# x added by VectorE, rotations of the scan on GpSimd, x scaled before its transposes, states used in groups of four

## The reference, cut to what matters

```python
h = rms_norm(x, norm_mix_g)
a_val, a_gate, u, g_conv, g_ssm = split(h @ w_in)              # 768, 768, 256, 1024, 1024 columns
v = silu(layer_norm(depthwise_conv31(a_val * sigmoid(a_gate)) + conv_b))
y_conv = v @ w_conv_out
s[t] = a * s[t-1] + B u[t]                                     # complex, 16 groups of 64 states
y = gelu(real(C s) + d_skip * u);  y_ssm = (y * sigmoid(y @ w_glu + b_glu)) @ w_ssm_out
x = x + (sigmoid(g_conv) * y_conv + sigmoid(g_ssm) * y_ssm) @ w_out
h = rms_norm(x, norm_ffn_g)
top_v, top_e = top_k(h @ w_router + b_router, 4);  gate = softmax(top_v)
for e in experts of a token:                                   # w_gate_up[e]: 1024 x 2048, w_down[e]: 1024 x 1024
    g, lin = split(h @ w_gate_up[e] + b_gate_up[e])
    x += gate_e * ((min(g, 7) * sigmoid(1.702 g) * (clip(lin, -7, 7) + 1)) @ w_down[e] + b_down[e])
out = rms_norm(x, norm_final_g)
```

## Time and profile before

| | us |
|---|---|
| median of three runs (lowest, highest) | 1112.43 (1111.92, 1113.12) |
| the profiled execution, its own time | 1112.21 |
| its span | 1110.5 |
| busy in the span: TensorE, VectorE, ScalarE, GpSimd | 1060.8, 284.6, 165.6, 75.3 |
| HBM traffic over the span | 389 GB/s, 432 MB |

### The profile page before, as it was taken

The page is one execution under the profiler, slowest core; times in us unless marked ns, Lnnn a source line. Parts: engine busy times, 40 slices in busy tenths (PEclk is TensorE's granted clock), DMA queues, the critical chain, the costliest instruction groups (busy, mean ns, idle before and its releaser), DMA issues.

```text
span 1110.5 us, 12064 instructions
## 1 busy us (share of the span) xinstructions
PE 1060.8 (96%) x4951; PEld 457.2 (41%) x4952; DVE 284.6 (26%) x661; ACT 165.6 (15%) x296; POOL 75.3 (7%) x153
## 2 busy tenths in 40 slices
PE   7999999999999999999999999999999999999996
PEld 6888784533333333333333333333333333333332
DVE  6999751311111111111111111111101111111112
ACT  3011301211111111111111111101001111111103
POOL 3975000000000000000000000000000000000000
PEclk9999999999999999999999999999999999999999
DMA  7853488799999999999999999999999999999995
GB/s 226 281 158 146 185 347 358 285 427 426 431 436 427 432 431 431 434 433 433 428 432 432 429 432 431 432 432 430 433 432 431 433 431 431 429 431 428 422 423 235
DMA packets 43035, 432.07 MB, mean 389 GB/s; under 512 B 5647, under 2 KB 21437, under 8 KB 24604
## 3 DMA queue, kind: packets, MB, share of 16 engines
q1 hardware_dynamic: 43004, 431.64, 92.9%
HBM read 430.58 MB, written 1.05 MB: 389 GB/s over the span
## 4 chain that ended last, share of the span: by engine, by line
PE 60%; DMA 26%; DVE 10%; ACT 1%; issue 1%; another core or an unknown queue 1%; SPq 1%; DVEq 0%
PE bank L1483 30%; DMA ring<-w_gate_up 22%; PE bank L1495 13%; DVE bank L936 6%; PE bank L1504 4%; PE bank L1445 4%; DMA ring<-w_down 3%; PE bank L1410 2%; PE bank L1375 2%; ACT area L722 1%; PE bank L1451 1%; PE bank L1476 1%; DVE bank L971 1%; DMA ring<-ssm_b_im 1%
## 5 line engine op out<-in xcount | busy, mean ns | idle before, releaser
L1483 PE MATMUL bank<-ring,area 128*64 128x512 f32 x2048 | 455.9, 602 | 22.3 <-DMA ring<-w_gate_up 22.3
L1483 PEld LDWEIGHTS bank<-ring,area 128*64 128x64 f32 x2048 | 149.4, 139 | 311.8 <-issue 272.5
L1495 PE MATMUL bank<-ring,area 128*64 128x512 f32 x1024 | 227.4, 595 | 6.1 <-ACT area L722 2.6
L1102 DVE TENSOR_SCALAR area<-bank 128x512 f32<-128x512 f32 x32 | 22.1, 692 | 732.6 <-PE bank L1483 732.6
L1495 PEld LDWEIGHTS bank<-ring,area 128*64 128x64 f32 x1024 | 72.0, 137 | 141.2 <-issue 131.7
L1264 PE MATMUL bank<-area,ring 128*128 128x256 f32 x480 | 106.6, 381 | 2.2 <-DMA ring<-w_in 2.2
L1264 PEld LDWEIGHTS bank<-area,ring 128*128 128x128 f32 x480 | 90.3, 190 | 17.1 <-DMA ring<-w_in 2.7
L728 ACT ACTIVATE area<-area 128x512 f32<-128x512 f32 x32 | 20.2, 632 | 486.9 <-DVE area L1102 486.9
L936 DVE SCALAR_TENSOR_TENSOR bank<-ring,spread,bank 128x256 f32<-128x256 f32 x174 | 71.5, 483 | 0.6
L1445 PE MATMUL bank<-rows,pick 128*64 128x512 f32 x256 | 63.6, 618 | 0.4 <-DVE onehot L1091 0.4
L1504 PE MATMUL bank<-area,spT 64*128 64x512 f32 x248 | 61.6, 615 | 0.7 <-ACT area L725 0.7
(11 more groups left out here) (243 smaller groups left out, 492.3 us busy)
## 6 DMA issues: line engine op xcount, KB each, us to landing
ring<-w_gate_up SPq DMA_DIRECT2D x47, 4096.0 KB, 48.9
ring<-w_down SPq DMA_DIRECT2D x26, 4096.0 KB, 46.6
ring<-w_gate_up SPq DMA_DIRECT2D x19, 2048.0 KB, 18.3
ring<-w_gate_up SPq DMA_DIRECT2D x30, 1024.0 KB, 12.0
ring<-w_down SPq DMA_DIRECT2D x18, 1024.0 KB, 21.2
ring<-w_in SPq DMA_DIRECT2D x15, 1024.0 KB, 8.0
ring<-w_down SPq DMA_DIRECT2D x3, 2048.0 KB, 10.8
ring<-w_out SPq DMA_DIRECT2D x1, 4096.0 KB, 14.2
```

The lines of the kernel that those rows point to most:

```text
L1102: return v.tensor_scalar(gc, bank[4][:, :], 7.0, None, ALU.min)
L1483: last = mm(bank[4 + b][64 * h:64 * h + 64, :], heT[:, k % 4, k // 4 * 64:k // 4 * 64 + 64], fours(w, b, h), start=False, stop=(k == KD - 1))
L1495: last = mm(bank[b][64 * h:64 * h + 64, :], src[:, k % 4, k // 4 * 64:k // 4 * 64 + 64], w[:, k % 2, h * 512:h * 512 + 512], start=(k == 0 ...
```

## The change

What it does, from the front to the end:

- VectorE and ScalarE scale one tile of x each by its reciprocal root into `x_rows`, TensorE transposes that, and the two engines share the eight blocks of hT, with the gain alone. A few products without use (`keep_busy`) stand where the transposes stood. One more small DMA brings norm_ffn_g into the parameter rows.
- VectorE writes the second product of a scan step into `rot`, and GpSimd takes the two sums of step t-1 behind its turning of step t; the last step's stay with VectorE. TensorE uses the states in two groups of four (`y_quad`).
- The gain of the second norm goes into w_router (`wrt_ready`, on VectorE ahead of the SSM gating) and, for the experts, into the copy of the transposed tokens (`by_gain_T`, VectorE instead of ScalarE). The broadcast of norm_ffn_g over all partitions is gone; w_router, b_router and the gain are issued behind w_out. Rows, logits and masks no longer lie in the slots of expert 1's chunks 6 to 8, which are issued earlier.
- x is no longer put into the banks by TensorE before the output products: VectorE adds it to their sums (`add_rows`), and the sum goes into the banks by four identity products (`residual`) behind expert 15. The output products of tile 1 run one half of the columns after the other, and its transposes and logits in two parts.
- Tokens are gathered with a stride, and ScalarE's copy `hrow` undoes it. Expert 27 is loaded in sets of four chunks.

```diff
-END = {E - 5: (4, 2, 2, 4), E - 4: (4, 2, 2, 4), E - 3: (4, 2, 1, 1, 4),
+END = {E - 4: (4, 2, 2, 4), E - 3: (4, 2, 1, 1, 4),
...
-WARM = 8, 2, 6, 3
+WARM = 1, 4, 6, 3
...
+        rot = [grid(at(23, 512, 512 * i), 2, T) for i in range(2)]
         ygelu, yglu = grid(at(11, 512), 2, T), grid(at(11, 512, 512), 2, T)
...
+            sp.dma_start(par_rows[r0:r0 + KD, :], norm_ffn_g[0].rearrange("(k p) -> k p", p=128)).then_inc(par_in, 16)
...
             sp.wait_ge(y_pe, ST)
-            sp.dma_start(gffn, norm_ffn_g.to_broadcast([128, D])).then_inc(ffn_in, 16)
-            sp.dma_start(wrt, w_router[0].rearrange("(p k) n -> p k n", p=128)).then_inc(ffn_in, 16)
-            sp.dma_start(brow, b_router.to_broadcast([128, E])).then_inc(ffn_in, 16)
+            load(1, 7, 1)
+            load(1, 8, 1)
...
             load_over_win((3, 4, 5, 0))
             sp.wait_ge(biasb_ready, 1)
             sp.dma_start(wout, w_out[0].rearrange("(k p) n -> p k n", p=128)).then_inc(wout_in, 16)
+            sp.dma_start(wrt, w_router[0].rearrange("(k p) n -> p k n", p=128)).then_inc(ffn_in, 16)
+            sp.dma_start(brow, b_router.to_broadcast([128, E])).then_inc(ffn_in, 16)
+            sp.dma_start(gain[:, :], norm_ffn_g[0].rearrange("(p k) -> p k", p=128)).then_inc(ffn_in, 16)
             load_over_win((1, 2))
             for h in range(2):
                 sp.dma_start(bdown[h], b_down[0, :, h * 512:h * 512 + 512]).then_inc(down_in, 16)
...
             load(1, 9, 1)
+            sp.wait_ge(mixed, 4)
+            load(1, 6, 1)
             for j in (1, 2, 3, 4):
                 sp.wait_ge(wout_used, j)
                 load(1, j, 1)
             load(1, 5, 1)
-            sp.wait_ge(logits_pe, TT)
-            load(1, 6, 1)
-            sp.wait_ge(top8, TT)
-            load(1, 7, 1)
-            sp.wait_ge(gates_ready, TT)
-            load(1, 8, 1)
...
+                if t >= 1:
+                    pool.wait_ge(rot_ready, t)
+                    x_, r_ = xs[(t - 1) % NX], rot[(t - 1) % 2]
+                    g.tensor_tensor(x_[:, 0, :], x_[:, 0, :], r_[:, 1, :], ALU.subtract)
+                    g.tensor_tensor(x_[:, 1, :], x_[:, 1, :], r_[:, 0, :], ALU.add).then_inc(states, 1)
 
...
+            act.wait_ge(rstd_x, 1)
+            s.activation(x_rows[:, 0, :], x_sb[:, 0, :], ACT.Copy, scale=rstd[:, 0:1]).then_inc(x_scaled, 1)
             act.wait_ge(params_pe, 1)
             s.activation(par[:, :], bank[7][:, 0:54], ACT.Copy).then_inc(params_sb, 1)
-            act.wait_ge(spread_pe, 1)
-            s.activation(rstd_all, bank[6][:, 0:T], ACT.Copy).then_inc(rstd_sb, 1)
...
+            for b in (1, 3):
+                act.wait_ge(xT_pe, b + 1)
+                for k in (2 * b, 2 * b + 1):
+                    s.activation(hT[:, k, :], bank[b][:, k % 2 * T:k % 2 * T + T], ACT.Copy, scale=p_g[:, k:k + 1]).then_inc(hT_act, 1)
...
+            square(0, 0)
+            square(0, 1)
+            act.wait_ge(h2T_pe, 1)
+            s.activation(h2T[:, 0:4, :], grid(bank[4][:, :], 4, 128), ACT.Copy).then_inc(h2T_act, 1)
+            root_and_exp(0)
+            s.activation(area[:, 1464:1466], ident[:, 0:2], ACT.Sqrt)
+            square(1, 0)
+            act.wait_ge(h2T_pe, 3)
+            act.wait_ge(logits_pe, 1)
+            s.activation(h2T[:, 0:4, :], grid(bank[6][:, :], 4, 128), ACT.Copy).then_inc(h2T_act, 1)
+            square(1, 1)
+            act.wait_ge(h2T_pe, 4)
+            s.activation(h2T[:, 4:6, :], grid(bank[7][:, 0:256], 2, 128), ACT.Copy).then_inc(h2T_act, 1)
+            root_and_exp(1)
+
...
-                return s.activation(hrow, bank[6][:, :], ACT.Copy)
-
-            def h_T_copy():
-                return s.activation(heT, grid(bank[7][:, :], 4, 128), ACT.Copy)
+                return s.activation(grid(hrow, 4, 128), bank[6][:, :].rearrange("a (p m) -> a m p", m=4), ACT.Copy)
...
-            link(v.reciprocal(rstd, rstd))
-            dve.wait_ge(consts, 1)
-            for t in range(TT):
-                v.tensor_scalar(diag[:, t, :], ident[:, :], rstd[:, t:t + 1], None, ALU.mult).then_inc(diag_ready, 1)
+            v.reciprocal(rstd, rstd).then_inc(rstd_x, 1)
+            dve.wait_ge(rstd_x, 1)
+            v.tensor_scalar(x_rows[:, 1, :], x_sb[:, 1, :], rstd[:, 1:2], None, ALU.mult).then_inc(x_scaled, 1)
...
-            dve.wait_ge(rstd_sb, 1)
-            for k in range(KD):
-                v.scalar_tensor_tensor(hT[:, k, :], bank[k // 2][:, k % 2 * T:k % 2 * T + T], p_g[:, k:k + 1],
-                                       rstd_all, ALU.mult, ALU.mult).then_inc(hT_ready, 1)
+            for b in (0, 2):
+                dve.wait_ge(xT_pe, b + 1)
+                for k in (2 * b, 2 * b + 1):
+                    v.tensor_scalar(hT[:, k, :], bank[b][:, k % 2 * T:k % 2 * T + T], p_g[:, k:k + 1], None, ALU.mult).then_inc(hT_dve, 1)
...
+                dve.wait_ge(rawT_pe, 1)
+                if t >= 1:
+                    dve.wait_ge(rot_ready, t)
...
+                if t >= 2:
+                    dve.wait_ge(states, t - 1)
...
                 v.tensor_tensor(xs[t % NX], zz, cb, ALU.mult)
-                link(v.tensor_tensor(zz, zz, sb_, ALU.mult))
-                v.tensor_tensor(xs[t % NX][:, 0, :], xs[t % NX][:, 0, :], zz[:, 1, :], ALU.subtract)
-                v.tensor_tensor(xs[t % NX][:, 1, :], xs[t % NX][:, 1, :], zz[:, 0, :], ALU.add).then_inc(states, 1)
-
+                v.tensor_tensor(rot[t % 2], zz, sb_, ALU.mult).then_inc(rot_ready, 1)
+                if t == ST - 1:
+                    dve.wait_ge(rot_ready, ST)
+                    v.tensor_tensor(xs[t % NX][:, 0, :], xs[t % NX][:, 0, :], rot[t % 2][:, 1, :], ALU.subtract)
+                    v.tensor_tensor(xs[t % NX][:, 1, :], xs[t % NX][:, 1, :], rot[t % 2][:, 0, :], ALU.add).then_inc(states, 1)
                 taps_of(order[scanning + SCAN_TAPS * t:scanning + SCAN_TAPS * (t + 1)])
-                dve.wait_ge(states, t + 1)
...
             v.tensor_copy(biasb[0:32, :], bias32[0:32, :]).then_inc(biasb_ready, 1)
+            dve.wait_ge(ffn_in, 48)
+            v.tensor_tensor(wrt, wrt, gain_k.unsqueeze(2).to_broadcast([128, KD, E]), ALU.mult).then_inc(wrt_ready, 1)
...
-            def weighed_by_k(t):
-
...
-                    v.tensor_tensor(dst[:, p, :], grid(gffn[:, c], 64, KD), grid(bank[2 * t + h][:, :], 64, KD),
-                                    ALU.mult).then_inc(h_ready, 1)
+            def add_rows(t, h):
+
+                r = rows[:, t, h * 512:h * 512 + 512]
+                v.tensor_tensor(r, bank[2 * t + h][:, :], r, ALU.add).then_inc(h_ready, 1)
...
+            def by_gain_T():
+
+                both = gain[:, :].rearrange("p (h m) -> p m h", h=2).unsqueeze(3).to_broadcast([128, 4, 2, CAP])
+                return v.tensor_tensor(heT.rearrange("p m (h c) -> p m h c", h=2),
+                                       bank[7][:, :].rearrange("p (m h c) -> p m h c", m=4, h=2), both, ALU.mult)
...
+                keep_busy(4)
+            pe.wait_ge(x_sq, TT)
+            keep_busy(2)
+            pe.wait_ge(par_in, 16 * 10)
...
+            tr(bank[7][:, 0:62], par_rows[:, :], ident[0:62, 0:62]).then_inc(params_pe, 1)
+            pe.wait_ge(x_scaled, TT)
+            for k in range(KD):
+                for t in range(TT):
+                    last = tr(bank[k // 2][:, k % 2 * T + t * 128:k % 2 * T + t * 128 + 128],
+                              x_rows[:, t, k * 128:k * 128 + 128], ident[:, :])
+                if k % 2:
+                    last.then_inc(xT_pe, 1)
...
-            y_pair(0)
+            y_quad(0)
             project(12)
-            y_pair(2)
             project(13)
-            y_pair(4)
             project(14, (0,))
-            y_pair(6)
-
+            y_quad(4)
...
-                if j == 1:
-
-                    pe.wait_ge(ssm_gated, 4)
-                    for n in range(4):
-                        mm(bank[n][:, :], ident[:, :], x_sb[:, n // 2, n % 2 * 512:n % 2 * 512 + 512], start=True, stop=False)
...
             pe.wait_ge(wout_in, 16)
-            pe.wait_ge(ffn_in, 48)
-            for t in range(TT):
+            pe.wait_ge(wrt_ready, 1)
+            pe.wait_ge(ssm_gated, 4)
...
+            def out_product(t, k, h):
+
+                pe.wait_ge(mixed, k // 2 + 1)
+                return mm(bank[2 * t + h][:, :], gateC[:, k, t * 128:t * 128 + 128], wout[:, k, h * 512:h * 512 + 512],
+                          start=(k == 0), stop=(k == KD - 1))
+
+            for k in range(KD):
+                for h in range(2):
+                    last = out_product(0, k, h)
+            last.then_inc(x1_pe, 1)
+            for h in range(2):
                 for k in range(KD):
-                    pe.wait_ge(mixed, k // 2 + 1)
-                    for h in range(2):
...
+                    last = out_product(1, k, h)
+                    if h == 1 and k % 2:
                         last.then_inc(wout_used, 1)
...
+                    if (h, k) == (0, 3):
```

(10 more changed lines are left out.)

233 lines of the change are left out of this document (112 added, 121 removed).

## The result

The changed kernel takes 1117.44 us (median of 5 runs, 1116.33 to 1117.78), the kernel before 1112.55 (1111.92 to 1113.12): ratio 1.0043, 95% interval 1.0033 to 1.0054. It is slower by 4.9 us; the forecast was 1.4 faster. The profiled execution took 1116.33, span 1114.5, so 4.0 more span than before.

What follows compares the result with a forecast made beforehand. The weight stream at 431 GB/s, started by expert 0's first refill, sets the end. Terms +0.1 + 1.7 + 0.45 - 2.6 - 1.2 + 0.15 = -1.4 on 1112.2, plus 0.2 for the median, gave 1111.0 us; range 1103.0 to 1115.5.

Steps and rivals of the forecast that it cites:

- The end follows the first refill one for one: Loop: every microsecond by which expert 0 starts earlier or later moves the end by one.
- That just fits: Scan steps: with two more sums GpSimd needs 5.5 us of a 5.65 us period; 5.5 us leave VectorE.
- my fourth: Rival, front: groups run two wide, GpSimd delays VectorE; TensorE 0.9 instead of 2.7 us earlier, 1112.8 us; chance 0.12.
- Groups of four: State products on TensorE: two groups of four at 1.1 us replace four pairs, 1.7 us saved.
- The added wait: Ahead of the SSM gating: ffn_in lands 2 us after w_out, output products start at 166.1; of 6.1 us gained, 0 left.
- Output products +2.15: Output products: +1.7 us for the lower clock after idleness, +0.45 for four transposes moved ahead of their end.
- Tail and gather, -2.6 - 1.2 + 0.15: Behind the output products: router's tail -2.6 us, first gather at full clock -1.2, strided hrow copy and scaled transposes +0.15.
- The loop and the early chunks at 0: Expert loop: TensorE's slack covers the added work, and the three chunks loaded earlier bring nothing.
- -2.7 + 2.8 + 2.15 - 3.65 = -1.4: The whole sum in us: front, added wait, output products, then tail and gather.
- faster, same and slower: Chances for the whole time: below 1110.2 us 0.40, between 0.45, above 1114.6 us 0.15.
- the four cases: The forecast (0.62), nothing late (0.14, 1103.2 us), short runs (0.12, 1116.0), the change not doing what it says (0.12, 1112.8).

Runs made afterwards that it cites:

- e7: The changed kernel with the edits of e6 and e3 together: 1104.66 us, ratio 0.9931.
- e2: The changed kernel with the scan's decay read from a PSUM bank from scan step 4 on: 1118.91 us, ratio 1.0066.
- e6: The changed kernel with the decay of all eight scans read from PSUM: 1111.72 us, ratio 0.9998.
- e1: The changed kernel with the rotation's two sums back on VectorE in all steps, the product staying in SBUF: 1121.04 us, ratio 1.0084.
- e9: e7 with VectorE's wait ahead of scan step 5 for the seventh copy of the scan's inputs instead of the eighth: 1105.82 us, ratio 0.9947.
- e10: e9 with the state products in four pairs instead of two groups of four: 1107.12 us, ratio 0.9953.
- e4: The changed kernel with 8 filler products on TensorE ahead of the second group of four and 9 behind it: 1114.44 us, ratio 1.0030.
- e3: The changed kernel with VectorE's wait for ffn_in and its w_router product behind the four mixes, TensorE's wait at the first logits: 1110.68 us, ratio 0.9992.
- e8: The changed kernel with the three small DMAs (w_router, b_router, gain) issued ahead of w_out instead of behind it: 1113.94 us, ratio 1.0019.

## Why the prediction was wrong

- **"The end follows the first refill one for one": right here.** +4.8 us of refill, +4.9 of time, 431 GB/s in the loop. Over the experiments it holds only roughly: e7's first refill is issued at 205.91, 13.5 us earlier than the changed kernel's, and its span is 11.0 shorter (1103.5).
- **The front, "That just fits": the step that failed.** I charged GpSimd's two sums with their own 1.5 us and looked only at whether GpSimd had room for them. I priced nothing for VectorE's instructions beside it. By that account 7 x 0.79 = 5.5 us are saved, and six scan pairs at about 2.59 instead of 1.27 take 7.9: +2.4, seen as +2.15 in the last scan (119.07 against 116.92). The mean product starts at 126.63, not 121.8. Shown by e2, where the two kinds of scan stand in one run, by e6, and by the second sum of e1. The Trainium skill has the rule, in "SBUF — State Buffer", section "Who interferes with whom": a VectorE instruction with two SBUF inputs contends with a GpSimd instruction that reads SBUF, and one with at most one does not, outside the 2-port modes. The traces agree: scan pairs go from 1.27 to 2.59 and the second sum from 0.41 to 1.49, while taps stay at 3.22 and scans with a decay in PSUM at 1.27. The first sum of e1 is the exception. It should have been a rival; my fourth, "GpSimd delays VectorE", meant only its own queue.
- **Groups of four: right, and a trap.** 16 passes take 1.07 us, as 8 did; e9 against e10 puts the saving at 2.3 us where I had 1.7. But with VectorE as the bound, the time that they save turns into 2.37 and 3.04 us of idleness around the second group, where before only 1.22 stood, and the mean product ran at half clock: +2.6, a term absent from my sum. I had charged this very effect behind the wait, but not here. Shown by e4. Together the front is 7.5 us off: 2.7 earlier was forecast for the end of the mean product, and it ends 4.8 later.
- **The added wait: right in its mechanism, +1.2 us overpriced.** w_out landed 14.3 us after its issue as forecast. ffn_in came 0.7 us behind it, not 2: w_router landed 13.2 us after its issue, a little ahead of w_out, while b_router's issue held SP for 9.51 us, and gain, issued last, landed 4.39 us later. So the short runs of w_router, for which I had charged the 2 us, did not delay ffn_in; the late issue of the gain did, by 0.7. From w_out's issue to the output products I had 20.6 us, it is 19.4. e3 gives 6.8 (6.3) us for the whole wait, 6.1 gained and eaten plus 1.7 of clock being my estimate.
- **Output products +2.15: +2.4** (64 passes of 628 ns on average against 593, and the transposes).
- **Tail and gather, -2.6 - 1.2 + 0.15: -4.2.** From the end of the output products to the gather it is 7.6 us instead of 10.3, -2.65; the gather takes 1.96 instead of 3.60 (both from the chains), -1.6; the rest, to expert 0's first product, +0.1. Expert 0 starts at full speed (13.75 us for its 64 passes, before and after), where I had let part of the low clock fall on it. The strided copy of hrow costs nothing (598 ns, 0.60 before).
- **The loop and the early chunks at 0: right**, no difference from the first refill on.

In my terms: -2.7 + 2.8 + 2.15 - 3.65 = -1.4; measured 4.9 + 1.7 + 2.4 - 4.2 = 4.8. The smaller misses, 1.1 us on the wait and 0.5 on the tail, went the other way and hid part of the front's.

The chances were rounded: their parts give 0.39, 0.47 and 0.14 for faster, same and slower, not 0.40, 0.45 and 0.15. None of the four cases had the front later than before.

Open is what holds SP in b_router's issue: it is there whenever w_out and w_router are ahead of it (8.3 to 11.9 us in all twelve such kernels) and gone in e8. But SP is held on a later issue then: three chunks of w_gate_up took 8.15 us to issue in e8, and 14.74 in the kernel before, also behind w_out. Room in the queue is a likely cause, and the 1,024 short runs of w_router may help to fill it; neither was tested, the latter because no run has w_router in long runs behind w_out. Open too is why w_out lands 13.2 to 16.6 us after its issue.

## What to carry to other kernels

Before work goes to GpSimd, list what VectorE runs beside it, and where its inputs lie: two in SBUF cost both engines here, one in PSUM did not (for casts see below); a wait that kept them apart may be the reason why the trace of before shows nothing. A step that makes TensorE faster but not the engine that it waits for can cost more than it saves, by the clock behind the idleness; fillers are the cheap cure. A wait belongs at its last possible place on an in-order engine: moving one by some 40 lines was worth 6.8 (6.3) us.

## What the hardware showed that I had not expected

- Conversions and memsets meet too: beside VectorE's cast of 96x2048 (1.22 us), GpSimd's memset of 128x128 took 1.22 us and its select 2.26 beside a subtraction of 2.29. In the kernel before, beside VectorE's taps, the same two took 0.20 and 0.29. VectorE kept its own times there; nobody waited for GpSimd.

```profile
144.81 1.22 POOL L610 MEMSET area<- 128x128 f32 x1 [27.43 <-DVE ring L1027]
146.11 2.26 POOL L612 TENSOR_SCALAR_AFFINE_SELECT area<-area 128x128 f32<-128x128 f32 x1
```

- The issue of one small DMA of 16 KB held SP for 9.51 us, and with it every issue behind it.
- The scan costs the same with its decay in PSUM as with it in SBUF and no GpSimd beside: 680 and 681 ns (medians, e2 and the kernel before).
